# Router logits by column groups: the router weight stationary, the tokens moving

## The reference

```
h2     = rms_norm(x, norm2_gain)                       # 256 x 1024
logits = einsum('sd,de->se', h2, w_router) + b_router  # 256 x 32
top_val, top_idx = top_k(logits, 4)                    # 4 of 32 experts per token
gates  = softmax(top_val)                              # scattered back to 256 x 32
out    = sum_e combine[:, e] * (act(h2 @ w1[e] + b1[e]) @ w2[e] + b2[e])
```

## Time and profile before

| | before |
|---|---|
| median of 3 timed runs | 1082.01 us (1081.59, 1082.01, 1085.42) |
| span of the profiled execution | 1080.7 us; the page gives no time of this execution besides it |
| TensorE busy | 1039.1 us, 96% |
| TensorE weight loads | 400.2 us, 37% |
| VectorE busy | 302.9 us, 28% |
| ScalarE busy | 157.1 us, 15% |
| GpSimd busy | 22.5 us, 2% |
| read from memory | 426.80 MB, 397 GB/s over the span |
| mean granted clock of TensorE | 0.986 |

### The profile page before, as it was taken

One profiled execution on the slowest core, in us unless ns is written; L12 is line 12 of the kernel. 1 busy time (PEld: TensorE's weight loads), 2 busy tenths in 40 slices (PEclk: granted clock), 3 DMA queues, 4 the chain that ended last, 5 costly groups with the idle time before them and its releaser, 6 DMA issues.

```text
span 1080.7 us, 11540 instructions
## 1 busy us (share of the span) xinstructions
PE 1039.1 (96%) x4616; PEld 400.2 (37%) x4616; DVE 302.9 (28%) x704; ACT 157.1 (15%) x282; POOL 22.5 (2%) x29
## 2 busy tenths in 40 slices
PE   8999999999999999899998999898989899999997
PEld 7458454333333333233333333233333233333332
DVE  2455622422222222132221222221323222221231
ACT  1231333110101111101010111011101101111112
POOL 1212000000000000000000000000000000000000
PEclk9999999999999999999998999999999999999999
DMA  9886947999999999999999999999999999999995
GB/s 326 241 245 268 379 176 317 384 432 412 431 431 431 431 428 432 434 429 431 428 429 431 435 430 428 434 433 432 429 433 433 432 429 434 432 432 431 425 429 230
DMA packets 33050, 429.79 MB, mean 398 GB/s; under 512 B 4892, under 2 KB 6336, under 8 KB 16352
## 3 DMA queue, kind: packets, MB, share of 16 engines
q1 hardware_dynamic: 31104, 426.03, 93.6%
q10 hardware_dynamic: 1216, 1.70, 1.1%
q0 software_dynamic: 704, 1.71, 0.6%
HBM read 426.80 MB, written 2.62 MB: 397 GB/s over the span
## 4 chain that ended last, share of the span: by engine, by line
PE 70%; DMA 27%; DVE 1%; SPq 1%; issue 1%; ACT 0%; DVEq 0%
PE ps L1361 31%; DMA w1r<-w_mlp 22%; PE ps L1389 13%; PE ps L1430 5%; PE ps L1110 4%; PE ps L1339 3%; PE ps L1098 3%; DMA w2r<-w_mlp 2%; DMA w1r<-w_out 1%; PE ps L1157 1%; PE ps L1263 1%; PE ps L1232 1%; PE ps L1403 1%; DMA w1r<-w_in 1%; PE ps L1347 1%; PE ps L1369 1%
## 5 line engine op out<-in xcount | busy, mean ns | idle before, releaser
L1361 PE MATMUL ps<-w1r,arena 128*64 128x512 f32 x2040 | 484.9, 611 | 22.4 <-DMA w1r<-w_mlp 22.0
L1361 PEld LDWEIGHTS ps<-w1r,arena 128*64 128x64 f32 x2040 | 141.8, 139 | 285.8 <-issue 279.6
L1389 PE MATMUL ps<-w2r,arena 128*64 128x512 f32 x960 | 212.0, 593 | 7.3 <-DMA w2r<-w_mlp 7.3
L1389 PEld LDWEIGHTS ps<-w2r,arena 128*64 128x64 f32 x960 | 68.0, 137 | 147.1 <-issue 131.4
L981 DVE TENSOR_TENSOR acc<-ps,acc 128x512 f32<-128x512 f32 x56 | 36.1, 686 | 175.1 <-PE ps L1430 175.1
L973 DVE TENSOR_TENSOR arena<-arena 128x512 f32<-128x512 f32 x32 | 22.2, 692 | 163.5 <-ACT arena L593 163.4
L935 DVE TENSOR_TENSOR arena<-ps,cols 128x512 f32<-128x512 f32 x31 | 21.4, 692 | 139.3 <-PE ps L1347 139.3
L597 ACT ACTIVATE arena<-ps 128x512 f32<-128x512 f32 x31 | 18.5, 597 | 288.4 <-PE ps L1369 288.3
L1339 PE MATMUL ps<-h,arena 128*64 128x512 f32 x248 | 58.7, 592 | 0.0
L602 ACT ACTIVATE arena<-ps 64x512 f32<-64x512 f32 x29 | 17.2, 592 | 269.5 <-PE ps L1389 269.5
L1430 PE MATMUL ps<-arena 128*128 128x512 f32 x112 | 55.5, 618 | 0.0
(11 more groups left out here) (257 smaller groups left out, 579.4 us busy)
## 6 DMA issues: line engine op xcount, KB each, us to landing
w1r<-w_mlp SPq DMA_DIRECT2D x54, 4096.0 KB, 30.9
w2r<-w_mlp SPq DMA_DIRECT2D x32, 2048.0 KB, 18.7
w2r<-w_mlp SPq DMA_DIRECT2D x14, 4096.0 KB, 20.8
w1r<-w_mlp SPq DMA_DIRECT2D x17, 2048.0 KB, 10.3
w1r<-w_in SPq DMA_DIRECT2D x7, 2048.0 KB, 17.1
w1r<-w_mlp SPq DMA_DIRECT2D x12, 1024.0 KB, 8.3
w1r<-w_out SPq DMA_DIRECT2D x2, 2048.0 KB, 13.7
rel_table<-arena ACTq DMA_DIRECT2D x1, 1536.0 KB
```

Source lines behind the costliest of these rows:

```text
L1361: ins = mm(ps[64 * c:64 * c + 64, 2 * par + n, :], hgT[:, par, k % 4, 64 * (k // 4):64 * (k // 4) + 64], cols_z, start=False, stop=(k == 7))
L1389: ins = mm(ps[at:at + 64, 4 + c, :], actT[:, k % 4, 64 * (k // 4):64 * (k // 4) + 64], w2r[:, k // 2, col:col + 512], start=(k == 0), stop ...
```

## The change

`route(t)` makes the router weights stationary and moves the tokens. Of the eight blocks of 128 in the width, four are taken at a time, each on its own group of 32 columns of the array: group g takes blocks g and 4 + g. The result is four partial sums, each transposed (32 experts by 128 tokens), on the 128 partitions of one PSUM bank. They are copied into SBUF (`lgT`), for tile 0 by ScalarE, for tile 1 by VectorE. A new function `route_sum(t)` multiplies this 128 x 128 block, stationary, with the constant `pick`, which adds the four groups and turns the result back to 128 tokens by 32 experts, at the place where the logits were before. On TensorE route_sum(0) stands behind the second half of project(1,1), route_sum(1) right behind route(1). The counts of `route_mm` change with it: 1 and 3 are the partial sums, 2 and 4 the logits. `choose(t)` waits for the logits, the load at L303 for count 3.

```diff
+        lgT = carve(arena, 2048, [TT, P])
...
-            sp.wait_ge(route_mm, 2)
+            sp.wait_ge(route_mm, 3)
             sp.dma_start(w1_extra, w1_v[0, 1, 1, :, 2048:4096]).then_inc(w1_in[3], 16)
...
             square_half(1, 0)
+            act.wait_ge(route_mm, 1)
+            nc.scalar.activation(lgT[:, 0, :], ps[:, 7, 0:P], ACT.Copy).then_inc(lgT_sb, 1)
             x2T_out(1)
...
             def choose(t):
-                dve.wait_ge(route_mm, t + 1)
+                dve.wait_ge(route_mm, 2 * t + 2)
...
             x2T_out(1)
+            dve.wait_ge(route_mm, 3)
+            v.tensor_copy(lgT[:, 1, :], ps[:, 0, 0:P]).then_inc(lgT_sb, 1)
             norm2(1)
...
             def route(t):
-                for k in range(KD):
-                    if k == 0:
-                        pe.wait_ge(x2T_act, t + 1)
-                    if k == 4:
-                        pe.wait_ge(x2T_dve, t + 1)
-                    ins = mm(ps[:, 6 - 3 * t, 0:NE], x2T[:, k, P * t:P * t + P], wr[:, k, :], start=(k == 0), stop=(k == KD - 1))
+                for j in range(2):
+                    pe.wait_ge((x2T_act, x2T_dve)[j], t + 1)
+                    for g in range(4):
+                        ins = mm(ps[32 * g:32 * g + 32, 7 - 7 * t, 0:P], wr[:, 4 * j + g, :], x2T[:, 4 * j + g, P * t:P * t + P],
+                                 start=(j == 0), stop=(j == 1))
                 ins.then_inc(route_mm, 1)
+
+            def route_sum(t):
+                pe.wait_ge(lgT_sb, t + 1)
+                mm(ps[:, 6 - 3 * t, 0:NE], lgT[:, t, :], pick, start=True, stop=True).then_inc(route_mm, 1)
...
             route(0)
             project(1, 1, range(2, 4))
+            route_sum(0)
             x2_T(1, 0)
...
             route(1)
+            route_sum(1)
```

More of the change, by code:

```diff
@@ L196, in hybrid_block @@
         first_half = sem("first_half"); norm2_ready = sem("norm2_ready"); first_pick = sem("first_pick"); first_made = sem("first_made"); first_copied = sem("first_copied")
-        ranked = sem("ranked")
         xt_done = sem("xt_done"); hT_ready = sem("hT_ready")
@@ L214, in hybrid_block @@
         half_mm = sem("half_mm"); out_mm = sem("out_mm"); x2_ready = sem("x2_ready")
-        h2_ready = sem("h2_ready"); x2_tr = sem("x2_tr"); x2T_act = sem("x2T_act"); x2T_dve = sem("x2T_dve"); wr_ready = sem("wr_ready"); route_mm = sem("route_mm")
+        h2_ready = sem("h2_ready"); x2_tr = sem("x2_tr"); x2T_act = sem("x2T_act"); x2T_dve = sem("x2T_dve"); wr_ready = sem("wr_ready"); route_mm = sem("route_mm"); lgT_sb = sem("lgT_sb")
         top_ready = sem("top_ready"); ex_done = sem("ex_done"); chosen_ready = sem("chosen_ready")
```

## The result

Over 20 runs of each, the changed kernel has a median of 1085.29 us (1080.38 to 1090.88) against 1082.13 us (1081.15 to 1085.42). The ratio is 1.0024, with a 95% interval of 1.0015 to 1.0034: 0.24% slower, which is less than the 0.5% named in the prediction. (The quotient of the two medians is 1.0029.) What stands out is the spread. The fastest run of the changed kernel is faster than any of the 20 of the kernel before; 9 of its 20 are over 1085.5, which none of before is.

A forecast was written before the change was run, and what follows sets the result against it. Bound by a weight stream at the memory's rate, its start set by the routing chain; 0.54 + 0.09 = +0.63 us on the 1080.7 span gives 1081.3, or 1082.6 as measured time; range 1081.2 to 1085.2.

The forecast's parts named there:

- sign of being wrong: First expert product before 172.75, a hole around the router groups, or its distance to the end changed by over a us.
- Where it counts: Start of the first expert product (L1361, 172.75 us): delay before it delays the weight stream and its end by as much.
- swallowed: Rival: the weight stream, with DMA at 0.99 to 1.00 from 173 us, absorbs the shift; 1082.0 us, chance 0.14.
- The groups in 0.72 us: Router part: 16 column-group instructions take 0.72 us instead of 1.71, from 8 taking 0.36 in the gate transposition (L1412).
- no overlap: Rival: the router's column groups don't overlap, 16 instructions still take 1.71 us; +2.2 us, 1084.2, chance 0.08.
- The bound of 0.43: Router part: low bound for the 16 column-group instructions, 0.43 us, a quarter of 1.71.
- A drain at each change of shape: Rival: TensorE drains at four tile-shape changes around the router parts, 0.27 us each; +1.1 more, 1083.7, chance 0.07.
- VectorE's order, +0.54: First tokens: VectorE does choose(0) before residual(1,1), which starts at about 165.08 instead of 164.54; 0.54 us lost.
- Tokens 128 to 255, +0.09: From the end of VectorE's copy L861 to the choice L867: 1.27 us instead of 1.18, 0.09 more.
- The sum, +0.63: Whole span: 0.54 plus 0.09 gives +0.63 us on 1080.7; bounds +0.04 to +2.56; time 1082.6.
- the clock rival: Rival: waits in the routing stage drop the granted clock to 1.2 GHz, slower by over 0.5%; 1088.0 us, chance 0.03.
- my rule: Before 173 us: the weight stream's start is late by half of the time spent at the lower clock level.

The follow-up runs named there:

- e2: Kernel before with the router cut to products 0 and 4 of the eight, no column groups; median 1080.36 us, ratio 0.9977.
- e8: Changed kernel with each set of four column-group products replaced by one full-shape product, logits not the router's; median 1085.72 us over five runs, ratio 1.0036.
- e4: Kernel before with the change for tokens 128 to 255 only; median 1082.62 us, ratio 1.0001.
- e1: Changed kernel with identity products, results never read, queued at three places where TensorE waits; median 1082.86 us, ratio 0.9998.
- e5: Changed kernel with route_sum(0) between the third and fourth product of project(1,1) instead of behind the fourth; median 1083.16 us, ratio 1.0005.

## Why the prediction came out as it did

The change lies within 0.5%, as forecast, and on the side forecast, a small loss. Its size is off: the ratio is 2.6 us (1084.7 against the median of before), four times the 0.63 of the sum, and the changed kernel's own median, 1085.29, is 0.09 above the end of the range. That the change still came out within the 0.5% is in good part luck: most of the loss comes from a mechanism to which I had given a chance of 0.03. The prediction's own sign of being wrong was met too: the distance from the first expert product to the end was not to change by more than a us, and it grew by 1.8 (1080.7 - 172.75 before, 1085.3 - 175.58 now). Point by point:

- *Where it counts.* Right about the stream: its start sets the end, one to one (4.57 and 4.6; after L353 the same 906.0). Not right that the start of L1361 alone decides: 1.74 of the loss lies between it and the first row released. The rival "swallowed" is refuted by this and by e2.
- *The groups in 0.72 us.* 0.57 for 16. The rival "no overlap" is wrong. The bound of 0.43 was too low.
- *A drain at each change of shape.* The Trainium skill's rule (TensorEngine Tiling (Array Packing), Key Properties) shows at most a small price here: the next projection begins at 160.98, right on 160.40 + 0.57, and its four instructions take 1.91 us, against 1.81 before and 1.72 in e8, where no shape changes. A drain can have cost 0.1 to 0.2 us there at most. The +0.46 of the whole path leaves no room for the 1.1 us of the rival.
- *VectorE's order, +0.54.* Right in mechanism. L851 follows on the choice and not on the projection, which had ended by 162.89. The size is half: the residual ends 4.53 us after route(0) begins (164.32 + 0.61 - 160.40), before 4.24, so +0.29. The choice began 0.12 us earlier than in my sum (the groups were 0.15 and the sum product 0.06 quicker, the projection 0.10 slower), L851 came right behind it without the 0.04 that I had put there, and it takes 0.61 in the chain instead of 0.70.
- *Tokens 128 to 255, +0.09.* From the end of VectorE's copy of x to the choice e4 has 166.79 to 168.12, 1.33 us for 1.18: +0.15.
- *The sum, +0.63.* +0.46 on the lead at full clock (e1). The 1082.86 measured there lies near the forecast 1082.6, but the kernel before had 1082.87 on that chip.
- *The step that failed* is the clock rival. I put it as one case with a threshold, "passes 5.4 us if the lower level lasts 11 us or more", at 0.03, and left every shorter fall out of the other cases. In the profiled execution the lower level lasted from 166.8 to 180.4 us, 13.6 us. It cost 2.97 us of the lead (15.18 - 12.21) and 1.74 behind it, 4.7 in all, and the span grew by 4.6. By my rule (half of the time spent at the lower level) it would have been 6.8. The rest cost nothing, since part of the slower work of TensorE took the place of its waits: e1's chain goes through VectorE's choice and ranks of the second tokens (the two lines below are the first and the last of them), and the changed kernel's chain is on TensorE all the way from 167.26 to 174.98. My argument against it, that the clock was 1.00 in 164 to 173 before, where TensorE was idle 0.68 of 9 us, was no evidence: I had myself counted 2 us more of waits in the new stage. I had read the waits as time and not as a cause.

```profile
167.98 0.26 DVE arena L869
...
169.91 0.33 DVE arena L880
```

The forecast also took one execution for the kernel. The lower level lasted 13.6 us in one execution and 6.8 in another; where it lasts differently long, the median is that of a mixture.

## What to carry to other kernels

Work taken from TensorE on a chain need not be a gain if what is left are waits: a few products that nobody reads, put where it waits and short enough hardly to delay what follows, gave about 3 us back here, with the chain otherwise unchanged. When a product is shortened by a detour through another engine, look first at what that engine had done ahead of the next item in its order: here the choice had been 0.54 us ahead of the projection and came to stand in front of it. And give a case of the clock its own part of the range at every length, not a threshold.

## What the runs showed of the hardware

- 16 instructions of 128x32 stationary and 128 moving on four column groups take 0.57 us, against 1.71 for 16 of 128x128 stationary and 32 moving: a factor of 3.0. In e8 four instructions of full shape (128x128 stationary, 128 moving), which do as many multiplications as those 16, take 0.45 us.
- The granted clock has two levels in this stage, 1.00 and 0.50; values between are windows with a change inside. It fell after a stretch in which TensorE was busy 4.06 of 6 us (changed kernel) and 3.96 of 6 (e8), stayed with 5.78 (e1), and in e5 stayed in the profiled execution with 4.97 of 6 (162 to 168). In the changed kernel it stayed low for 13.6 us in one execution and 6.8 in another, though TensorE was busy for 11.81 of the 12 us from 168 to 180 in the first and without a pause from 168 to 172 in the second.
- A wait of 0.5 to 1.3 us near the kernel's start, at 14 us, is followed in 4 of 12 profiled executions by some 3.4 us at the lower level, which cost 1.6 to 1.7 us in the next group of products.
